# Plain first and second weight tiles behind each layer norm, the first by token halves, in a two-block transformer kernel

## The reference

```python
# first block, for each layer l
mix = token_mixer(h, w_in[l], ...)             # h @ w_in: 1024 x 3072, then attention, then @ w_o
h = layer_norm(ALPHA * h + mix, ln1_g[l], ln1_b[l])
q = (h @ w_query[l]).reshape(T, 8, 2, 128)     # queries of 8 heads
scores = einsum('thpc,hpnc->thpn', q, sub_keys[l])
top_s, top_i = top_k(scores, 16)               # then the best 16 of the pairs, softmax gates
ffn = sum over chosen e of gate_e * gelu(h @ expert_u[l][e]) * expert_v[l][e]
h = layer_norm(ALPHA * h + ffn, ln2_g[l], ln2_b[l])
# second block, for each layer l
x = layer_norm(ALPHA * x + hybrid_mixer(x, ...), ln_g[l, 0], ln_b[l, 0])
x = layer_norm(ALPHA * x + memory_cross_attention(x, mem, ...), ln_g[l, 1], ln_b[l, 1])
y = square(relu(x @ mlp_w_up[l])) @ mlp_w_down[l]
x = layer_norm(ALPHA * x + y, ln_g[l, 2], ln_b[l, 2])
```

## Time and profile before

| what | value |
|---|---|
| median of 3 runs | 3021.17 us (3020.09 to 3023.12) |
| profiled execution, its own time | 3018.93 us |
| its span | 3017.1 us |
| PE busy | 2921.2 us, 97% |
| PE weight loads busy | 2499.5 us, 83% |
| DVE (VectorE) busy | 2024.4 us, 67% |
| ACT (ScalarE) busy | 1348.2 us, 45% |
| POOL busy | 147.1 us, 5% |
| mean granted TensorE clock | 0.993 |
| ring transfers, median from issue to landing | 464 of 1 MB, 4.8 us |

### The profile page before, as it was taken

One profiled execution on the slowest core, in us unless ns is written; L12 is line 12 of the kernel. 1 busy time (PEld: TensorE's weight loads), 2 busy tenths in 40 slices (PEclk: granted clock), 3 DMA queues, 4 the chain that ended last, 5 costly groups with the idle time before them and its releaser, 6 DMA issues. The chain is left out here.

```text
span 3017.1 us, 50691 instructions
## 1 busy us (share of the span) xinstructions
PE 2921.2 (97%) x19226; PEld 2499.5 (83%) x19226; DVE 2024.4 (67%) x3838; ACT 1348.2 (45%) x2045; POOL 147.1 (5%) x76
## 2 busy tenths in 40 slices
PE   8999999999999999899999999999998999999898
PEld 7688888899888877888889988889876888887687
DVE  4489866788667647997678875774635666563666
ACT  4442444444444544334444444445534444552543
POOL 0052000000000004400000000010000001000000
PEclk9999999999999999999999999999999999999999
DMA  5243355544555524425554455554333555334454
GB/s 214 89 179 131 124 195 181 195 154 152 190 186 188 188 98 168 140 100 194 186 190 168 140 194 182 207 184 166 112 135 144 186 190 188 137 110 153 162 187 153
DMA packets 68019, 493.52 MB, mean 164 GB/s; under 512 B 7576, under 2 KB 7584, under 8 KB 8352
## 3 DMA queue, kind: packets, MB, share of 16 engines
q1 hardware_dynamic: 67568, 490.42, 45.0%
q0 software_dynamic: 304, 1.06, 0.1%
HBM read 490.39 MB, written 1.06 MB: 163 GB/s over the span
## 5 line engine op out<-in xcount | busy, mean ns | idle before, releaser
L860 ACT ACTIVATE tile_h<-ring 128x1024 fp32r<-128x1024 f32 x644 | 646.7, 1052 | 802.3 <-PE ps L791 442.3
L909 DVE TENSOR_TENSOR ring_l<-ring,tile_h 128x1024 fp32r<-128x1024 f32 x648 | 764.0, 1220 | 359.1 <-ACT tile_h L860 354.7
L711 PE MATMUL ps<-x_hl,tile_h 128*128 128x512 f32 x1504 | 530.2, 398 | 1.6 <-issue 1.6
L713 PE MATMUL ps<-x_hl,ring_l 128*128 128x256 f32 x1504 | 421.5, 280 | 0.0
L711 PEld LDWEIGHTS ps<-x_hl,tile_h 128*128 128x128 f32 x1504 | 282.5, 188 | 72.0 <-issue 2.3
L713 PEld LDWEIGHTS ps<-x_hl,ring_l 128*128 128x128 f32 x1504 | 283.8, 189 | 0.2
L789 PE MATMUL ps<-tile_h,w_odd 128*128 128x512 f32 x640 | 249.9, 391 | 4.0 <-DVE w_odd L933 4.0
L789 PE MATMUL ps<-tile_h,w_even 128*128 128x512 f32 x640 | 249.4, 390 | 3.6 <-DVE w_even L933 3.6
L790 PE MATMUL ps<-ring_l,w_odd 128*128 128x512 f32 x640 | 249.0, 389 | 0.0
L790 PE MATMUL ps<-ring_l,w_even 128*128 128x512 f32 x640 | 249.0, 389 | 0.0
L791 PE MATMUL ps<-tile_h,w_odd 128*128 128x512 f32 x640 | 249.0, 389 | 0.0
(11 more groups left out here) (340 smaller groups left out, 5872.5 us busy)
## 6 DMA issues: line engine op xcount, KB each, us to landing
ring<-stream SPq DMA_DIRECT2D x464, 1024.0 KB, 4.8
cs<-consts SPq DMA_DIRECT2D x1, 1712.5 KB, 8.5
x<-x_in SPq DMA_DIRECT2D x1, 1024.0 KB, 4.9
arena<-scratch POOLq DMA_DIRECT2D x1, 1024.0 KB, 7.7
out<-x SPq DMA_DIRECT2D x2, 512.0 KB, 2.6
tab<-table SPq DMA_DIRECT2D x1, 1.0 KB, 8.2
scratch<-arena POOLq DMA_DIRECT2D x1, 12.0 KB, 5.0
```

Source lines behind the costliest of these rows:

```text
L711: nc.tensor.matmul(both, uh[:, c, f], x_hl[:, :, c, :], start=(c == 0), stop=False, skip_group_check=True)
L713: ins = nc.tensor.matmul(bank[:, SEQ:2 * SEQ], ul[:, c, f], x_h[:, c, :], start=False, stop=(c == KC - 1), skip_group_check=True)
L860: nc.scalar.activation(tile_h[:, j % 2, n], slot(k + j)[:, n], ACT.Copy).then_inc(hi_ready, 1)
L909: nc.vector.tensor_tensor(low_of(k + j)[:, n], slot(k + j)[:, n], tile_h[:, j % 2, n].bitcast(F32), ALU.subtract).then_inc(lo_ready, 1)
```

## The change

- `up_as_turned` becomes `turned_tile`: tile 0 is multiplied plain by halves of 128 tokens. The two calls of `pe_turn_x` move into it: turning of tokens 0 to 127, their 16 products, turning of tokens 128 to 255, their 16 products. `arrived` of tile 0 stands ahead of it, as it did ahead of `up_as_turned`. At the memory query the turnings stay outside (`turn=False`), and `release` is called in the last chunk of the second half there and at the expert queries.
- At the projections and the MLPs tile 1 is now plain too (`second_tile`), over all tokens, in bank 5. `release` moves into it: behind the fourth chunk of its first feature half, just ahead of which the norm and small slots are given back; tile 0 is counted there too. The first split tile is tile 2 (`PROJ_A`, `PROJ_B` one smaller).
- The turned tokens go to banks 5, 6, 7 and 0 in place of 4 to 7; the memory values move to bank 1, and in the MLP the two pairs of banks change places (`flip`).
- ScalarE takes the high parts of tiles 2 and 3 ahead of emptying tile 0.
- At the expert queries tile 2 is plain too (`FIRST_WQ` 3), one tile fewer for POOL's low parts.
- The mirroring of the band moves from between the blocks to ahead of tile 6 of the second block's first projection, VectorE's sums of T to ahead of tile 7's low parts; POOL loads the band behind the last norm of the first block.

Cut to the changed lines, but for the first part:

```diff
@@ -286,17 +286,35 @@
             for which in range(len(tiles)):
                 some(1, 1, which).then_inc(tile_done, 1)
 
-        def up_as_turned(pe, m, w, bank, release):
+        TURNED = [5, 6, 7, 0]
+
+        def turned_tile(pe, m, w, bank, turn=True, release=None):
+
+            for tt in range(TT):
+                if turn:
+                    pe_turn_x(pe, m - 1 if m else None, [tt])
+                for c in range(KC):
+                    pe.wait_ge(xt_ready, 2 * KC * m + (KC * tt + c + 1))
+                    if release is not None and tt == TT - 1 and c == KC - 1:
+                        release()
+                    for fb in range(2):
+                        at = fb * SEQ + tt * P
+                        last = nc.tensor.matmul(ps[bank][:, at:at + P], w[:, c, fb * P:(fb + 1) * P],
+                                                xT[:, c, tt * P:(tt + 1) * P], start=(tt == 0 and c == 0 and fb == 0),
+                                                stop=(c == KC - 1), skip_group_check=True)
+            return last
+
+        def second_tile(w, bank, release):
 
             for fb in range(2):
                 for c in range(KC):
-                    if fb == 0:
-                        pe.wait_ge(xt_ready, 2 * KC * m + (KC + c + 1))
-                    if fb == 1 and c == KC // 2:
+                    if fb == 0 and c == 3:
                         release()
                     last = nc.tensor.matmul(ps[bank][:, fb * SEQ:(fb + 1) * SEQ], w[:, c, fb * P:(fb + 1) * P],
                                             xT[:, c, :], start=(c == 0), stop=(c == KC - 1))
-            return last
+                    if fb == 0 and c == 3:
+                        last.then_inc(tile_done, 1)
+            last.then_inc(tile_done, 1)
 
         def norm_read(pe, n):
             pe.wait_ge(ln_x, n * TT + TT)
@@ -308,9 +326,11 @@
+                    elif TURNED[2 * tt + g] == 0:
+                        pe.wait_ge(t_ev, 1)
...
-                        last = nc.tensor.transpose(ps[4 + 2 * tt + g][:, j * P:(j + 1) * P],
+                        last = nc.tensor.transpose(ps[TURNED[2 * tt + g]][:, j * P:(j + 1) * P],
@@ -632,7 +652,7 @@
-        FIRST_WQ = 2
+        FIRST_WQ = 3
@@ -998,12 +1017,14 @@
-            up_as_turned(pe, 2 * l, chunks(A_PROJ), 4, small_and_norm_read).then_inc(tile_done, 1)
+            turned_tile(pe, 2 * l, chunks(A_PROJ), 4)
+            arrived(pe, 1, l, A_PROJ + 1)
+            second_tile(chunks(A_PROJ + 1), 5, small_and_norm_read)
...
-            for j in range(1, 6):
+            for j in range(2, 6):
...
-                pe_project(pe, "features" if j < 4 else "tokens", A_PROJ, l * SPLIT_A - 1, j,
+                pe_project(pe, "features" if j < 4 else "tokens", A_PROJ, l * SPLIT_A - 2, j,
@@ -1111,7 +1132,6 @@
-            pe_turn_x(pe, l * 2)
@@ -1141,7 +1161,7 @@
-                        up_as_turned(pe, 2 * l + 1, chunks(A_WQ), 4, norm_and_keys_read)
+                        turned_tile(pe, 2 * l + 1, chunks(A_WQ), 4, release=norm_and_keys_read)
@@ -1204,12 +1224,12 @@
-            pe_turn_x(pe, l * 2 + 1)
...
-            act_high(act, 1, l, A_PROJ, 0, 1, free=True)
+            for j in range(2, 4):
+                act_high(act, 1, l, A_PROJ, 0, j, free=True)
@@ -1373,21 +1393,21 @@
-            for j in range(1, 3):
-                dve_low(dve, A_PROJ, l * SPLIT_A - 1, 0, j)
+            for j in range(2, 4):
+                dve_low(dve, A_PROJ, l * SPLIT_A - 2, 0, j)
...
-            for j in range(3, 7):
-                dve_low(dve, A_PROJ, l * SPLIT_A - 1, 0, j)
+            for j in range(4, 7):
+                dve_low(dve, A_PROJ, l * SPLIT_A - 2, 0, j)
...
-                    dve_low(dve, A_PROJ, l * SPLIT_A - 1, 0, 7)
+                    dve_low(dve, A_PROJ, l * SPLIT_A - 2, 0, 7)
...
-                    dve_low(dve, A_PROJ, l * SPLIT_A - 1, 0, 8)
+                    dve_low(dve, A_PROJ, l * SPLIT_A - 2, 0, 8)
...
-                    dve_low(dve, A_PROJ, l * SPLIT_A - 1, 0, 9)
+                    dve_low(dve, A_PROJ, l * SPLIT_A - 2, 0, 9)
@@ -1738,13 +1759,22 @@
-            up_as_turned(pe, norm, chunks(B_PROJ), 4, small_and_norm_read).then_inc(tile_done, 1)
+            turned_tile(pe, norm, chunks(B_PROJ), 4)
+            arrived(pe, 2, l, B_PROJ + 1)
+            second_tile(chunks(B_PROJ + 1), 5, small_and_norm_read)
...
-            for j in range(1, 11):
+            for j in range(2, 11):
+                if l == 0 and j == 6:
+                    pe.wait_ge(t_in, 16)
+                    for b in range(4):
+                        last = nc.tensor.matmul(ps[b][:, :], cs[:, CONST["flip"]],
+                                                band_in[:, 512 * b:512 * b + 512], start=True, stop=True)
+                    last.then_inc(t_flip, 1)
...
-                pe_project(pe, "features" if j < 7 else "tokens", B_PROJ, LAYERS * SPLIT_A + l * SPLIT_B - 1, j, 4 + j % 4).then_inc(tile_done, 1)
+                pe_project(pe, "features" if j < 7 else "tokens", B_PROJ, LAYERS * SPLIT_A + l * SPLIT_B - 2, j, 4 + j % 4).then_inc(tile_done, 1)
...
+            pe.wait_ge(t_ready, 1)
@@ -1899,32 +1929,33 @@
-            up_tokens(chunks(B_XV), chunks(B_MEM), 0).then_inc(tile_done, 2)
+            up_tokens(chunks(B_XV), chunks(B_MEM), 1).then_inc(tile_done, 2)
...
-            up_as_turned(pe, norm + 1, chunks(B_XQ), 4, lambda: norm_read(pe, norm + 1)).then_inc(tile_done, 1)
+            turned_tile(pe, norm + 1, chunks(B_XQ), 4, turn=False, release=lambda: norm_read(pe, norm + 1))\
+                .then_inc(tile_done, 1)
...
-            pe_turn_x(pe, norm + 1)
-            g, s = LAYERS * PAIRS + l * MLP_PAIRS, LAYERS * SPLIT_A + l * SPLIT_B - 1 + PROJ_B + GATE_B
+            g, s = LAYERS * PAIRS + l * MLP_PAIRS, LAYERS * SPLIT_A + l * SPLIT_B - 2 + PROJ_B + GATE_B
...
-            up_as_turned(pe, norm + 2, chunks(B_MLP), 4, lambda: norm_read(pe, norm + 2)).then_inc(tile_done, 1)
+            turned_tile(pe, norm + 2, chunks(B_MLP), 4)
+            arrived(pe, 2, l, B_MLP + 1)
+            second_tile(chunks(B_MLP + 1), 5, lambda: norm_read(pe, norm + 2))
...
-            for j in range(1, 4):
-                pe_up_wide(pe, B_MLP, s, sums, 0, j)
+            pe_up_wide(pe, B_MLP, s, sums, 0, 2, 1)
+            pe.wait_ge(u_act, g + 4)
+            pe_up_wide(pe, B_MLP, s, sums, 0, 3, 1)
...
-                    pe_up_wide(pe, B_MLP, s, sums, i, j)
+                    pe_up_wide(pe, B_MLP, s, sums, i, j, 1)
...
-            if l + 1 < LAYERS:
-                pe_turn_x(pe, norm + 2)
@@ -1932,11 +1963,11 @@
-            act.wait_ge(t_flip, 1)
...
-            act_high(act, 2, l, B_PROJ, 0, 1, free=True)
+            for j in range(2, 4):
+                act_high(act, 2, l, B_PROJ, 0, j, free=True)
...
-                if j + 2 < 11:
+                if 2 <= j < 9:
@@ -2077,7 +2107,15 @@
-                dve_low(dve, B_PROJ, LAYERS * SPLIT_A + l * SPLIT_B - 1, 0, j)
+                if l == 0 and j == 7:
+                    dve.wait_ge(t_flip, 1)
+                    for b in range(4):
+                        t_last = nc.vector.tensor_tensor(T[:, 2 * b:2 * b + 2, :],
+                                                         ps[b][:, :].rearrange("p (h k) -> p h k", h=2),
+                                                         causal.unsqueeze(1).to_broadcast([P, 2, 256]), ALU.add)
+                    t_last.then_inc(t_ready, 1)
+                    dve.wait_ge(t_ready, 1)
+                dve_low(dve, B_PROJ, LAYERS * SPLIT_A + l * SPLIT_B - 2, 0, j)
@@ -2230,7 +2266,7 @@
-            pool.wait_ge(tile_done, (LAYERS - 1) * A_TILES + (A_EXP + 7 * BLK + 1))
+            pool.wait_ge(ln_x, 2 * LAYERS * TT + TT)
@@ -2282,16 +2312,8 @@
-            pe_turn_x(pe)
...
-            pe.wait_ge(t_in, 16)
-
-            for b in range(4):
-                last = nc.tensor.matmul(ps[b][:, :], cs[:, CONST["flip"]],
-                                        band_in[:, 512 * b:512 * b + 512], start=True,
-                                        stop=True)
-            last.then_inc(t_flip, 1)
```

More of the change, by code:

```diff
@@ L698, in pe_up, with wide_bank, pe_up_wide @@
             ins.then_inc(tile_done, 1)
-        def wide_bank(j):
-            return 4 + 2 * (j % 2)
-        def pe_up_wide(pe, k, s, sums, i, j):
+        def wide_bank(j, flip):
+            return 4 + 2 * ((j + flip) % 2)
+        def pe_up_wide(pe, k, s, sums, i, j, flip=0):
             pe.wait_ge(lo_ready, 2 * s + 8 * i + (2 * j + 2))
@@ L707, in pe_up_wide @@
             for fb in range(2):
-                bank, f = ps[wide_bank(j) + fb], slice(fb * P, (fb + 1) * P)
+                bank, f = ps[wide_bank(j, flip) + fb], slice(fb * P, (fb + 1) * P)
                 both = bank[:, :].rearrange("p (x n) -> p x n", x=2)
@@ L721, in pe_wide_block, with dve_sum @@
                     pe_up_wide(pe, k, s, sums, i, j)
-        def dve_sum(dve, block, l, k, i, j):
+        def dve_sum(dve, block, l, k, i, j, flip=0):
```

(42 more changed lines are left out.)

23 lines of the change are left out of this document (8 added, 15 removed).

## The result

The changed kernel takes 3036.06 us (median of 5 runs, 3034.20 to 3038.94), the one before 3021.17 (5 runs, 3020.09 to 3023.12): 1.0049 times as long, with a 95% interval of 1.0038 to 1.0060. The forecast was 3042, with a range of 3027 to 3057. The profiled execution took 3034.2 us with a span of 3032.4, so 15.3 more than the span before, where the sum of the steps had said 21.3.

The account below looks back on a forecast made before the run. PE works almost throughout, so only its waits or product count matter. Start 4.6, queries 6.0, layer 1's projection 7.1, second block 7.3 and 3.1, memory queries 0.6, MLPs -7.4: +21.3 us, taken as 3042, range 3027 to 3057.

Parts of the forecast that it names:

- The held wait: First tile's `arrived` ahead of both turnings holds PE, and behind it ScalarE and VectorE, until the landing: 3.6 us.
- The first rival: Tile 0 has landed when PE reaches the turning, so turnings keep their old times: -7.4 us, 3014, chance 0.08.
- Layer 1's projection: First block: late landing, late release, and ScalarE emptying tile 0 late put tile 2 at 1033.1 against 1026.0: +7.1 us.
- Second block: Its two projections: tile 2 later by 3.7 and 3.1 us; with the band at full price, +7.3 in layer 0, +3.1 in layer 1.
- the sign: Ahead of a projection's tile 2, PE stands 3 to 6 us, in the second block released by VectorE's low half.
- The release: Norm tile's slot goes free at the second tile's fourth chunk, 1.3 us in, leaving 5.6 us of work as cover.
- Start: Kernel's first projection: tile 0 lands at 14.8, tile 0 is emptied at 34.8, against tile 2's old start 30.2: +4.6 us.
- Queries: Both WQ sites: VectorE's head search starts at 176.2 in place of 168.29; less pause and POOL's saving, +3.0 us each.
- Second rival: Head search: VectorE and POOL collide more, 15 us more, 3057, chance 0.15; or 15 us less, 3027, chance 0.05.
- the rival's lower case: Head search: the long colliding head of before is gone and 15 us come back: 3027, chance 0.05.
- MLP: Both MLPs: the first half fills the gap between turnings and tile 2 starts sooner: -3.7 us each, -7.4 together.
- Third rival: Tile 2 waits shorter: 6 us less at layer 1's projection, 2 at the start, 3 in second block: 3031, chance 0.14.

Follow-up runs that it names:

- the wait alone: Kernel before, with only the wait for the first tile put ahead of the turnings at the six sites whose tile is in flight: 3039.83 us against 3020.77.
- both turnings first: Changed kernel, with both turnings ahead of the wait for the first tile at six sites; token halves and release as changed: 3021.66 us.
- the MLPs alone: Kernel before, with the change made only at the two MLPs: 3011.84 us against 3020.45 for the kernel before.
- both edits: Changed kernel, both turnings ahead of the first tile's wait (six sites), tile 0 emptied before tile 3's high part and the exponential (first block's projections): 3014.43 us against 3018.88.

## Why the prediction was right, point by point

**The held wait** was the forecast's core, and it holds: first turnings at the landing (at the start at 14.92, forecast 14.8), 3.2 to 3.7 us of wait at the other five. The first rival, that the wait does not decide, is excluded by the wait alone (19.1 us) and by both turnings first (14.4). The Trainium skill's rule (DMA: Bandwidth & Descriptors, Rules for kernel authors), to wait on a transfer late, agrees with both.

**Layer 1's projection** was to cost 7.1 and cost 8.9. Tile 2 started at 1038.11, on the old axis 1032.9, where the step said 1033.1: wait, releaser and order were right. The term missed is the clock: 1.7 us were charged ahead of the turnings (the first half took 5.27 in place of 3.84), but nothing behind the second wait, which cost another 2.0. Inside the step two misses cancelled, which is luck: the slots' transfers were issued at 1025.34, on the old axis 1020.2 and 1.2 us sooner than the step's release, and the second of them landed 8.7 us after that and not 7.6.

**Second block.** The forecast had tile 2's low half on VectorE as what PE waits for, 3 us. The size came out smaller (tile 2 begins 2.1 and 2.4 us later than before, forecast 3.7 and 3.1), and the place did not come out: ahead of tile 2 PE stands 0 and 0.72 us where the sign said 3 to 6. I had counted POOL's transfer of the band into tile 2's landing, but not the copy of the small tile that stands behind it and behind the second turning, and PE meets it inside the second tile. The band's products were right: 3.6 us at full price.

**The release** was put "at the second tile's fourth chunk, 1.3 us in". It is not PE's position that decides but VectorE's norm and POOL's copy. Where those are done early, with both turnings first, the slot's transfer is issued ahead of the second tile's first product (at 1017.0, the product at 1018.12), so in this run the increment did not wait for the queued products.

**Start.** 4.6 forecast, 3.2 found: tile 2 began at 33.25, and the step said 34.8. The small tile's slot was given back sooner, ahead of the second tile's first product: the transfer was issued at 24.69 and not at 27.2, and landed 5.9 us later where the step had 4.8.

**Queries.** 3.0 each forecast, 2.0 and 2.2 found. The search of layer 0 starts at 178.65, on the old axis 175.5 (forecast 176.2) against 168.29. Of these 7.2 us 5.2 come back, 4.2 of them because the pause of the earlier trace rows is gone: in layer 0 the step that took the pause off was right. In layer 1 the same number came out by luck. Its search has no such pause before; it starts 7.5 us later in its stage, and the 4.4 us that come back (74.5 us from the first head's start to the eighth's before, 70.1 after) are sums that meet fewer splits, 22.8 us before and 18.3 after. Layer 1's sums, two lines before and two after:

```profile
L1462 DVE SCALAR_TENSOR_TENSOR arena<-arena 128x48 f32<-128x48 f32 x16 | 12.1, 754 | 0.0
L1459 DVE SCALAR_TENSOR_TENSOR arena<-arena 128x64 f32<-128x64 f32 x16 | 10.7, 669 | 0.0
L1482 DVE SCALAR_TENSOR_TENSOR arena<-arena 128x48 f32<-128x48 f32 x16 | 9.8, 613 | 0.0
L1479 DVE SCALAR_TENSOR_TENSOR arena<-arena 128x64 f32<-128x64 f32 x16 | 8.5, 534 | 0.0
```

The wrong sign was "PE's wait for it grows": in layer 0 the search ends 2.0 us later in its stage's time, and PE itself is later still, so its waits, both layers together, shrink from the 31.3 us of the earlier trace rows to

```profile
  DVE arena L1540: 28.2, 4
```

**Second rival.** A colliding head was to add or save 15 us over both layers; after, the 15.9 us head of layer 0 is gone, but others take 10.5 to 12.1, and the sums cost 18.4 us against 18.8 before: no net change there. In layer 1 the rival's lower case came in by 4.4 us, in place of the pause, which layer 1 does not have. That a phase can cost that much is shown by the run with two plain query tiles. What the Trainium skill says of a VectorE instruction with two SBUF inputs and a GpSimd one (SBUF — State Buffer, SBUF: two separate sides) agrees with sums of 0.20 and of 2.4 us.

**MLP.** -3.7 each forecast, -5.3 and -3.2 found, -8.6 together by the medians of the MLPs alone (forecast -7.4). The filled wait is the mechanism that was forecast. Tile 2 came where the step put it: 2355.07, on the old axis 2333.5. The 2 us by which layer 0 goes beyond layer 1 belong to the execution before, not to the change (last section); at one pace the change brings some 3.2 a layer, 6.5 together, a little less than forecast.

**Third rival**, shorter waits at tile 2, came in at the start, where the tile landed inside the second one, by 1.5 us, and in the second block by 1.6 and 0.7; not at layer 1's projection, which was the largest part of it.

## What to carry to other kernels

Filling a wait with half a tile pays only if the tile is there when the wait begins; look up the landing against the start of the wait, site by site, before one pattern is put everywhere. A wait that is moved ahead of a step also moves what hangs on that step on other engines (here ScalarE's root, VectorE's norm, POOL's copy and, by them, the next transfer). When two engines hold the same instruction, one edit alone shows little: take both away together before judging either.

## What the runs showed that I had not expected

At a granted clock of 1.00 the MLP's products ran at two paces, each steady through one layer's MLP: 183 records in 32 us in layer 0 of the execution before and of those with both edits, 186 in layer 0 of after and with the MLPs alone. Layer 0 after, and then with both edits:

```profile
2361.00:2393.00 32.00, 32.00 (x186) 27.95 (x186) 21.33 (x24) 15.19 (x18) 0.00 (x0) 1.00 0.55 197
```

```profile
2343.00:2375.00 32.00, 32.00 (x183) 27.74 (x182) 19.98 (x22) 13.81 (x17) 0.00 (x0) 1.00 0.53 193
```

The pace belongs neither to a kernel nor to a whole execution. Layer 1 of the execution before ran at the other one, and so did layer 0 of the kernel before with the wait held:

```profile
2844.00:2876.00 32.00, 32.00 (x186) 27.97 (x185) 20.18 (x24) 14.51 (x17) 0.00 (x0) 1.00 0.53 182
```

```profile
2360.00:2392.00 32.00, 32.00 (x186) 28.19 (x185) 19.93 (x24) 14.48 (x17) 0.00 (x0) 1.00 0.52 185
```

Over the some 90 us of a layer's wide products 1.6% make 1.5 us. That is what layer 0's stage takes more with both edits than after (184.32 against 182.8), and layer 1's, at the same pace in both, takes the same (193.06 and 193.02). It is also most of the 2.0 us between layer 0 before (188.09) and with the wait held (186.05). The instructions are the same there, so it isn't the change; what sets the pace stays open.

The clock did not fall behind every wait: at 0.50 behind 5.83 us, but at 1.00 behind the 1.85 us ahead of tile 2 in the second block of the kernel with both edits (2022 to 2024).
